# New opening for a two-layer diffusion backbone: modulation in four column bands of the PE array, in groups of 512 features, each group normalised, split and multiplied into two output tiles when it arrives

## Chip, cores, metric

One core of one Trainium2 chip. The time is the device time of one execution in microseconds; of two kernels the lower one is better. The engines have one in-order list of instructions each: PE (TensorE, matmuls), DVE (VectorE), ACT (ScalarE), POOL (GpSimd) and SP (SyncE, which here only issues DMAs). They wait for one another with semaphores.

## What is computed

Two layers over 256 latent and 256 context tokens (512 columns, T) of width 2048, all in float32:

```python
for i in range(2):
    sh_l, sc_l, g_l = split(silu(c)     @ ada_w[i] + ada_b[i], 3)   # ada_w[i]: 2048 x 6144
    sh_c, sc_c, g_c = split(silu(c_ctx) @ ada_w[i] + ada_b[i], 3)
    u_lat = rmsnorm(h_lat, norm_g[i]) * (1 + sc_l) + sh_l
    u_ctx = rmsnorm(h_ctx, norm_g[i]) * (1 + sc_c) + sh_c
    o_lat, o_ctx = mixer_i(u_lat, u_ctx)       # begins with u @ w_in (2048 x 6656, layer 1: 2048 x 4416)
    h_lat = h_lat + g_l * (o_lat @ w_out[i])   # and h_ctx in layer 0
return h_lat
```

Layer 0 mixes with windowed attention and a Hyena branch, whose filters (`z -> sin -> sin -> w3 * decay`) and their spectra don't depend on the tokens; they are made in the opening. Layer 1 mixes with two kinds of attention. What matters here is the way up to the first products `u @ w_in` of each layer.

## The kernel before

**Layout.** Tokens lie transposed, `hT[128, 16, 512]`: 16 feature tiles (k) of 128 partitions, 512 token columns. A product makes one output tile of 128 features: the weights are cast to a high part `wh` (ACT, `split_high`, L810) and a low part `wl` (DVE, `split_low`, L820), the normed input likewise to `xh` and `xl`, all of type fp32r, and PE adds `wh.xh + wh.xl` over 16 k's (L836, L839) and then `wl.xh` (L842): 48 matmuls of 512 columns. Weights arrive in `raw`, `wh` and `wl` hold two tiles each. Layer 0 has 52 tiles, its output projection 16, layer 1 has 41 slots, its projection 16 (half as wide).

**Blocks.** The program is a sequence of blocks, between which all engines wait for each other: `start_block`, `norm_block` of layer 0, `layer0_block`, `out_block`, `norm_block` of layer 1, `layer1_block`, `out_block`.

**`start_block`.** The modulation `silu(c) @ ada_w` for c and c_ctx at once. Of layer 0's 6144 columns, 2048 (the scale, chunks 2 and 3) go through PE: pieces of 128 x 1024 as the moving operand, the two conditioning vectors in 8 columns of weights (`condw`, L527), into one bank, turned to columns afterwards. The others, and layer 1's, go by chunks of 1024 columns through DVE (`ada_piece`, L338 and L350: multiply a piece by one number per partition and add, once for each vector; `ada_fold`, `ada_columns` L389 and `ada_store` L400 then sum over partitions). Chunks 0 and 1 (the shift) are done in this block, 32 pieces of 512 KB loaded by POOL (L362, a ring of two); the other eight in later blocks, two pieces per output tile. Beside that: PE turns the token rows (`xtok`) to `hT` (L519, ACT copies, L554), POOL squares and sums them (L684, L686), and four filters are made in four stages each (`filters`: matmuls with w3 L489; decay L618; sums of magnitudes L501 of `flt_abs` L560; reciprocal L635; spectra L509; scaling L642; bias L650; stores to `spectra`).

**`norm_block`.** One matmul sums the squares over partitions (L725), ACT takes the root (L732), DVE the reciprocal of 128x512 (L758). Then for each k: `ntmp = hT * nri` (POOL L720, every third on DVE L772), scale and shift (ACT, two halves, L745), cast to `xh` and difference to `xl` (DVE, L764, L766), and PE runs the products of the first tile on what arrives. SP stores `hT` as the residual, 4 MB.

Of the kernel before, what the change touches and what calls it, by code (L numbers as in the profile page):

```python
# [31 lines left out]
P = 128  # L32
D = 2048
# [44 lines left out]


# [79 lines left out]
def sbuf_map(nc):  # L159
# [44 lines left out]
    b.xtok = put("xtok", "U", 0, [P, 4, D])  # L204
    b.w3 = put("w3", "U", 32 * K, [64, 4096])
    b.decay = put("decay", "U", 48 * K, [P, 2, BW])
    b.lag = put("lag", "U", 56 * K, [P, 2, 512])
    b.hT = put("hT", "S", 0, [P, KT, T])
    b.hybias = put("hybias", "S", 32 * K, [P, 2, BW])
    b.mlpw = put("mlpw", "S", 40 * K, [64, 384])  # L210
    b.zpos, b.w1, b.w2 = b.mlpw[0:33, 0:256], b.mlpw[0:33, 256:320], b.mlpw[:, 320:384]
    b.mlp0 = put("mlp0", "S", 42 * K, [64, 256])
    b.mlp1 = put("mlp1", "S", 43 * K, [64, 256])
    b.mlp2 = put("mlp2", "S", 44 * K, [64, 256])
    b.mlp3 = put("mlp3", "S", 45 * K, [64, 256])
    b.rows = put("rows", "HL", 0, [P, 3, P])
    b.flt = put("flt", "HL", 2 * K, [P, 4, 512])
    b.flt_s = put("flt_s", "HL", 10 * K, [P, 2, 512])
    b.flt_d = put("flt_d", "HL", 14 * K, [P, 2, 512])
    b.flt_abs = put("flt_abs", "EX", 0, [P, 2, 512])  # L220
    b.condw = put("condw", "V", 2560, [P, KT, 14])
    b.adarow = put("adarow", "S", 42 * K, [8, 512])
    b.flt_inv = put("flt_inv", "HL", 20 * K, [P, 512])
    b.kstage = put("kstage", "HL", 22 * K, [P, 4, 512])
    b.ada_w_pe = put("ada_w_pe", "RAW", 0, [P, 4, 1024])

    b.nsq = put("nsq", "EX", 4 * K, [P, T])
    b.nsum = put("nsum", "EX", 6 * K, [P, T])
    b.nrs = put("nrs", "S", 32 * K, [P, T])
    b.nri = put("nri", "S", 34 * K, [P, T])  # L230
# [77 lines left out]
ADA_START = 2  # L308
ADA_PE = 2
ADA_CHUNKS = [(0, n) for n in (0, 1)] + [(0, 4), (0, 5)] + [(1, n) for n in range(6)]  # L310
# [6 lines left out]


def ada_source(ada_w, layer, n, k):
    return ada_w[layer, k * P:(k + 1) * P, n * 1024:(n + 1) * 1024]  # L320
# [36 lines left out]
def ada_load(pool, b, s, ada_w, p):  # L357

    if p >= 2:
        pool.wait_ge(s.ada_used, p - 1)  # L360
    layer, n = ADA_CHUNKS[p // KT]
    pool.dma_start(b.ada_w[:, p % 2, :], ada_source(ada_w, layer, n, p % KT)).then_inc(s.ada_landed[p % 2], 16)  # L362


def ada_fold(nc, dve, b, s, chunk):
# [4 lines left out]
    if chunk > 0:  # L370
        dve.wait_ge(s.ada_summed, chunk)
# [22 lines left out]
def ada_store(nc, dve, b, s, bank, chunk):  # L394
# [3 lines left out]
    dve.wait_ge(s.ada_summed, chunk + 1)  # L398
# [3 lines left out]
        bias.unsqueeze(1).to_broadcast([P, vecs, 8]), ALU.add).then_inc(s.ada_stored, 1)  # L402


def start_block(nc, b, s, ps, g):
# [3 lines left out]
    with block:  # L409
# [3 lines left out]
        def _(sp):  # L413
            sp.dma_start(b.core[:, 0:2 * P], g.core[:, 0:2 * P]).then_inc(s.ident_in, 16)
            sp.dma_start(b.rows[:], g.rows).then_inc(s.rows_in, 16)
            sp.dma_start(b.mlpw[:], g.mlpw).then_inc(s.rows_in, 16)
            sp.dma_start(b.sink[:], g.ev_sink.to_broadcast((P, HEADS))).then_inc(s.rows_in, 16)
            for t in range(4):
                src = (g.x, g.ctx)[t // 2][0, (t % 2) * P:(t % 2 + 1) * P, :]
                sp.dma_start(b.xtok[:, t, :], src).then_inc(s.x_in, 16)  # L420

            def store_spectra(f):

                o, c = f // 2, f % 2
                sp.wait_ge(s.k_scaled, 4 * (f + 1))
                sp.wait_ge(s.k_ready, 2 * (f + 1))
                for h in range(2):
                    sp.dma_start(g.kf_d[2 * c + h, :, o], b.kstage[:, :, 256 * h:256 * h + 256]).then_inc(s.k_out, 16)

            for n in range(KT):  # L430
                for h in range(2):
                    p = 2 * n + h
                    if p >= 4:
                        sp.wait_ge(s.ada_pe_used, p - 3)
                    sp.dma_start(b.ada_w_pe[:, p % 4, :], ada_source(g.ada_w, 0, ADA_PE + h, n)).then_inc(
                        s.ada_pe_landed[p % 4], 16)
# [29 lines left out]
        def _(pe):  # L466
# [1917 lines left out]
```

## Time and profile before

| | |
|---|---|
| median of 3 runs | 1713.72 us (1712.8 to 1721.43) |
| the profiled execution | 1720.74 us, of which span 1719.0 us |
| PE busy | 1583.7 us, 92% of the span |
| DVE, ACT, POOL busy | 1153.0, 544.2, 294.5 us |
| mean granted PE clock | 0.953 of full speed |
| DMA | 279.62 MB, 163 GB/s in the mean |

Busy time of PE includes matmuls that run at half clock or use few columns of the array, so it is to be read stage by stage.

### The profile page before, as it was taken

To read this page: it belongs to the slowest core of one execution; us is meant where nothing else is said; L and a number is where in the kernel's file an instruction comes from. 1 tells how busy PE (TensorE), PEld (TensorE's weight loads), DVE (VectorE), ACT (ScalarE), POOL (GpSimd) and SP (SyncE) were. 2 spreads that over 40 slices of the span, in tenths; PEclk is the share of its full clock that TensorE was granted. 3 is DMA by queue.
4 is the path that set the end of the run, shared out by engine and by line. 5 is a ranking of instruction groups with operands and counts; after the bars stand their busy time and mean duration, and the time that the engine had idled before them with its cause. 6 is when DMAs were issued, how large, how long until landed. Compare 5 with 4: busy or idle time off the path is not lost. (4 is left out here: it accounts for less than half of the span.)

```text
span 1719.0 us, 19161 instructions
## 1 busy us (share of the span) xinstructions
PE 1583.7 (92%) x7619; PEld 1216.7 (71%) x7619; DVE 1153.0 (67%) x1244; ACT 544.2 (32%) x742; POOL 294.5 (17%) x296
## 2 busy tenths in 40 slices
PE   4998499999999999999999899968999988899998
PEld 1322168888878877887877688844788866688998
DVE  3898879988889758668675555547457656464543
ACT  1111332222222232332322311114336555554432
POOL 0233523232223100000000044432000000000000
PEclk9988679999999999999999999986999999999999
DMA  9786645655565554454445867741244324134575
GB/s 327 242 283 229 201 147 166 191 167 182 164 191 164 172 158 136 144 157 148 130 153 189 262 209 210 218 164 48 75 112 110 98 62 117 43 98 124 153 216 147
DMA packets 303224, 279.62 MB, mean 163 GB/s; under 512 B 13472, under 2 KB 267744, under 8 KB 301408
## 3 DMA queue, kind: packets, MB, share of 16 engines
q1 hardware_dynamic: 280096, 194.50, 38.1%
q0 software_dynamic: 23040, 83.90, 14.8%
q8 instruction: 61, 1.00, 0.2%
q14 instruction: 27, 0.22, 0.0%
HBM read 257.40 MB, written 20.97 MB: 162 GB/s over the span
## 5 line engine op out<-in xcount | busy, mean ns | idle before, releaser
L836 PE MATMUL banks<-xh,wh 128*128 128x512 f32 (+1 forms) x1904 | 674.3, 369 | 42.3 <-DVE xh L764 24.7
L839 PE MATMUL banks<-xl,wh 128*128 128x512 f32 (+1 forms) x1904 | 658.2, 360 | 8.9 <-DVE xl L766 7.9
L836 PEld LDWEIGHTS banks<-xh,wh 128*128 128x128 f32 x1904 | 367.5, 193 | 110.6 <-issue 45.4
L839 PEld LDWEIGHTS banks<-xl,wh 128*128 128x128 f32 x1904 | 367.5, 193 | 77.2 <-DVE xl L766 22.5
L842 PE MATMUL banks<-xh,wl 128*128 128x512 f32 (+1 forms) x1904 | 379.2, 352 | 0.0
L820 DVE TENSOR_TENSOR wl<-raw,wh 128x2048 fp32r<-128x2048 f32 (+1 forms) x124 | 282.4, 2277 | 110.6 <-ACT wh L810 110.6
L842 PEld LDWEIGHTS banks<-xh,wl 128*128 128x128 f32 x1904 | 315.5, 191 | 47.7
L810 ACT ACTIVATE wh<-raw 128x2048 fp32r<-128x2048 f32 (+1 forms) x124 | 235.4, 1899 | 252.4 <-PE banks L842 168.5
L338 DVE SCALAR_TENSOR_TENSOR ada_acc<-ada_w,cond,ada_acc 128x1024 f32<-128x1024 f32 x150 | 199.6, 1331 | 24.8 <-DMA ada_w<-in_ada_w 22.3
L362 POOL DMA_DIRECT2D ada_w<-in_ada_w x160 | 87.1, 544 | 706.6 <-DVE ada_acc L350 512.8
L350 DVE SCALAR_TENSOR_TENSOR ada_acc<-ada_w,cond,ada_acc 128x1024 f32<-128x1024 f32 x120 | 166.2, 1385 | 0.0
L2068 DVE RECIPROCAL rs<-rs 128x256 f32<-128x256 f32 (+1 forms) x27 | 56.9, 2108 | 57.9 <-ACT rs L1984 57.8
L1621 DVE SCALAR_TENSOR_TENSOR hT<-banks,ada,hres 128x256 f32<-128x256 f32 x48 | 21.8, 481 | 108.5 <-PE banks L842 108.5
L527 PE MATMUL banks<-ada_w_pe,condw 128*8 128x512 f32 x128 | 63.9, 646 | 6.9 <-DMA ada_w_pe<-in_ada_w 6.9
L1163 ACT ACTIVATE cx<-banks,cols 128x512 f32<-128x512 f32 x16 | 12.5, 778 | 149.0 <-PE banks L842 149.0
L969 POOL TENSOR_TENSOR spec<-spec,prod 128x512 f32<-128x512 f32 x32 | 47.7, 1515 | 59.6 <-DVE prod L1303 59.6
L684 POOL TENSOR_TENSOR nsq<-hT 128x512 f32<-128x512 f32 x30 | 47.3, 1578 | 18.1 <-DVE hT L1621 17.3
L686 POOL TENSOR_TENSOR nsum<-nsum,nsq 128x512 f32<-128x512 f32 x30 | 46.0, 1532 | 2.3
L2102 DVE TENSOR_REDUCE mx<-banks 128x2 f32<-128x1024 f32 x16 | 19.6, 1224 | 38.3 <-PE banks L1891 30.5
L554 ACT ACTIVATE hT<-banks 128x512 f32<-128x512 f32 x16 | 9.6, 598 | 112.3 <-PE banks L519 112.3
L527 PEld LDWEIGHTS banks<-ada_w_pe,condw 128*8 128x8 f32 x128 | 10.8, 94 | 48.5 <-issue 41.3
L745 ACT ACTIVATE nu<-ntmp,ada,gain 128x256 f32<-128x256 f32 x64 | 34.6, 592 | 31.1 <-DVE ntmp L772 12.8
(240 smaller groups left out, 1544.5 us busy)
## 6 DMA issues: line engine op xcount, KB each, us to landing
ada_w<-in_ada_w POOLq DMA_DIRECT2D x160, 512.0 KB, 4.2
raw<-in_ev_w_in SPq DMA_DIRECT2D x52, 1024.0 KB, 7.2
raw<-in_od_w_in SPq DMA_DIRECT2D x34, 1024.0 KB, 5.6
raw<-in_w_out SPq DMA_DIRECT2D x32, 1024.0 KB, 6.4
ada_w_pe<-in_ada_w SPq DMA_DIRECT2D x32, 512.0 KB, 6.6
residual<-hT SPq DMA_DIRECT2D x2, 4096.0 KB, 14.7
spectra<-kstage SPq DMA_DIRECT2D x8, 512.0 KB, 3.9
kf<-spectra SPq DMA_DIRECT2D x4, 1024.0 KB, 4.9
```

What stands on the lines that cost most here:

```text
L338: ins = nc.vector.scalar_tensor_tensor(out=acc[:, 0, :], in0=w, scalar=b.cond[:, k, 0:1], in1=acc[:, 0, :], op0=ALU.mult, op1=ALU.add)
L350: ins = nc.vector.scalar_tensor_tensor(out=acc[:, 1, :], in0=w, scalar=b.cond[:, k, 1:2], in1=acc[:, 1, :], op0=ALU.mult, op1=ALU.add)
L362: pool.dma_start(b.ada_w[:, p % 2, :], ada_source(ada_w, layer, n, p % KT)).then_inc(s.ada_landed[p % 2], 16)
L527: last = nc.tensor.matmul(ps[7][0:8, :], b.condw[:, n, 6 - 2 * q:14 - 2 * q], b.ada_w_pe[:, p % 4, 512 * x:512 * x + 512], start=(p == 0 a ...
L684: nc.gpsimd.tensor_tensor(b.nsq[:], x, x, ALU.mult).then_inc(s.squared, 1)
L810: nc.scalar.activation(b.wh[:, t % 2, 0:width], b.raw[:, t % 2, 0:width], ACT.Copy).then_inc(s.hi_done, 1)
L820: nc.vector.tensor_tensor(b.wl[:, t % 2, 0:width], b.raw[:, t % 2, 0:width], b.wh[:, t % 2, 0:width].bitcast(F32), ALU.subtract).then_inc( ...
L836: nc.tensor.matmul(out, wh[:, k, :], b.xh[:, seg, k, :], start=(k == 0), stop=False)
L839: nc.tensor.matmul(out, wh[:, k, :], b.xl[:, seg, k, :], start=False, stop=False)
L842: last = nc.tensor.matmul(out, wl[:, k, :], b.xh[:, seg, k, :], start=False, stop=(k == KT - 1))
L969: nc.gpsimd.tensor_tensor(b.spec[:, j], b.spec[:, j], b.prod[:, j % 2, :].rearrange("p (v c) -> p v c", v=2), ALU.subtract if j % 2 == 0 e ...
L2068: v.reciprocal(b.rs1[:, 0:width], b.rs1[:, 0:width]).then_inc(s.odd_rstd, 1)
```

## The change

- `start_block` loads layer 0's scale and shift (4096 columns) in 32 pieces of 1 MB, laid out beforehand so that every partition's part is one run of 8 KB: eight groups of 512 output columns, four pieces each, first the scale and then the shift of the features 0 to 511, then of the next 512. A piece has four k's; PE multiplies k number q of it into PSUM partitions 32q to 32q+31 (`ada_matmuls`), so a group's sum lies in four bands; ACT copies it to `arow`, and four small matmuls with `quads` turn it and add the bands (`ada_turn`). DVE adds the bias and makes the gain (`modulation`). Nothing of layer 0's scale and shift goes through DVE's sums any more.
- The work is written out by ticks, one per piece. The four filters start at ticks 2, 6, 11 and 15, a stage a tick; their magnitudes are also summed in bands. The spectra are stored unscaled, the inverse of the magnitude sums (128x4 a filter) is applied where layer 0 mixes; the bias is added to one row of the filter.
- Tokens are laid out as `hT` beforehand and loaded by POOL. ACT squares them at ticks 4 and 5, PE sums them (`square_sums`), the root and the reciprocal are taken of 128x4 and spread by PE into a bank; DVE multiplies `hT` by it in place.
- Group by group ACT shifts four k's (ticks 9, 17, 25 and at the end), DVE splits them, and PE adds them to two output tiles at once (`pair_product`): k's 0 to 11 at ticks 22 to 28, 12 to 15 at the end. `layer0_block` therefore starts its products at tile 2 (`if i > 1`), and the weights of tile 2 are split in the opening.
- `norm_block` is left for layer 1 alone: root and reciprocal of 128x4, spread by PE; DVE scales, ACT shifts and also casts to `xh`, DVE makes `xl`; PE makes tiles 0 and 1 together.
- All weight tiles of both layers and of both output projections are laid out beforehand, so that a tile is one run of 8 KB per partition and not 16 of 512 bytes. The residual of layer 0 is read from the input; its store is gone.

```diff
+def modulation_tiles(a):
+    first = a["ada_w"][0][:, :2 * D].reshape(4, 4, P, 2, 4, 512)
+    first = first.transpose(4, 3, 0, 2, 1, 5)[:, ::-1]
...
+FILTER_TICK = (2, 6, 11, 15)
+SQUARE_TICK = 4
+SPLIT_TICK = 20
+PAIR_TICK = {22: (0, 1), 23: (2, 3), 24: (4, 5), 25: (6, 7), 27: (8, 9), 28: (10, 11)}
+SCALE_TICK = {7: range(0, 6), 8: range(6, 12), 9: range(12, 16)}
...
+            for p in range(ADA_PIECES):
+                if p >= 3:
+                    sp.wait_ge(s.ada_pe_used, p - 2)
+                sp.dma_start(b.ada_ring[:, p % 3].rearrange("p k n -> p (k n)"), g.ada_first[p]).then_inc(
+                    s.ada_pe_landed[p % 3], 16)
...
+                if p == 12:
+                    load_raw(sp, b, s, 0, l0_weights(g, 0), (KT, P))
+                if p == 20:
+                    sp.wait_ge(s.flt_sd, 12)
+                    load_raw(sp, b, s, 1, l0_weights(g, 1), (KT, P))
...
+            def ada_matmuls(p):
+                grp, r = divmod(p, 4)
+                pe.wait_ge(s.ada_pe_landed[p % 3], 16 * (p // 3 + 1))
+                if r == 0 and grp > 0:
+                    pe.wait_ge(s.row_kept, rows_kept("ada", grp - 1))
+                for q in range(4):
+                    last = nc.tensor.matmul(ps[7][32 * q:32 * q + 32, :], b.condw[:, 4 * r + q, :], b.ada_ring[:, p % 3, q, :],
+                                            start=(r == 0), stop=(r == 3), skip_group_check=True)
+                last.then_inc(s.ada_pe_used, 1)
...
+            for tick in range(ADA_PIECES):
+                ada_matmuls(tick)
+                if tick == 0:
+                    pe.wait_ge(s.curved, 2)
+                    nc.tensor.matmul(ps[3][0:64, 0:256], b.w2, b.mlp3[:], start=True, stop=True).then_inc(s.mlp_mm, 1)
+                if tick % 4 == 0 and tick > 0:
+                    ada_turn(tick // 4 - 1)
+                if filter_stage(tick) is not None:
+                    filters(*filter_stage(tick))
+                if tick in (SQUARE_TICK, SQUARE_TICK + 1):
+                    for k in range(8 * (tick - SQUARE_TICK), 8 * (tick - SQUARE_TICK) + 8):
+                        square_sums(k)
...
+                if tick in PAIR_TICK:
+                    pe.wait_ge(s.norm_scaled, KT)
+                    pe.wait_ge(s.norm_root, 1)
+                    pe.wait_ge(s.hi_done, 2)
+                    pe.wait_ge(s.lo_done, 2)
+                    for k in PAIR_TICK[tick]:
+                        for i in range(2):
+                            pair_product(nc, pe, b, s, 0, i, k, ps[i], k + 1, k + 1)
+            ada_turn(ADA_GROUPS - 1)
+            for i in range(2):
+                for k in range(KT - 4, KT):
+                    last = pair_product(nc, pe, b, s, 0, i, k, ps[i], k + 1, k + 1)
+                last.then_inc(s.proj_done, 1)
...
+            for tick in range(ADA_PIECES):
...
+                if tick % 8 == 1 and tick > 8:
+                    shift(tick // 8 - 1)
+                if tick == SPLIT_TICK:
+                    act.wait_ge(s.k_out, 128)
+                    split_high(nc, act, b, s, 0)
+                    split_high(nc, act, b, s, 1)
...
+def pair_product(nc, pe, b, s, t, i, k, bank, high, low):
+    out = bank.rearrange("p (v t) -> p v t", t=256)
+    wh = b.wh[:, (t + i) % 2, :].rearrange("p (k m) -> p k m", m=P)
+    wl = b.wl[:, (t + i) % 2, :].rearrange("p (k m) -> p k m", m=P)
+    pe.wait_ge(s.norm_high, high)
+    nc.tensor.matmul(out, wh[:, k, :], b.xh[:, :, k, :], start=(k == 0), stop=False)
+    nc.tensor.matmul(out, wl[:, k, :], b.xh[:, :, k, :], start=False, stop=False)
+    pe.wait_ge(s.norm_low, low)
+    return nc.tensor.matmul(out, wh[:, k, :], b.xl[:, :, k, :], start=False, stop=(k == KT - 1))
...
 def l0_weights(g, i):
     col = l0_tile(i)[1]
-    return g.ev_w_in[0, :, col:col + P].rearrange("(k p) n -> p k n", p=P)
+    return g.ev_tiles[col // P].rearrange("p (k n) -> p k n", k=KT)
...
-                if i > 0:
+                if i > 1:
                     product(nc, pe, b, s, i, ps[i % 2])
...
-                    v.tensor_tensor(out, out, gate, ALU.mult).then_inc(s.mixed, 1)
+                    v.scalar_tensor_tensor(out=out, in0=out, scalar=b.inv_sum[:, o, 2 * grp + c:2 * grp + c + 1], in1=gate,
+                                           op0=ALU.mult, op1=ALU.mult).then_inc(s.mixed, 1)
```

## Rows read from the trace of the kernel before

**Rows 1.** Busy time by stage: us, then each engine busy (x), PEclk, DMA share, GB/s.

```profile
22.60:187.20 164.60, 138.14 (x337) 43.57 (x337) 131.31 (x122) 19.56 (x34) 55.70 (x59) 0.90 0.70 239
...
187.20:234.80 47.60, 29.19 (x50) 13.72 (x50) 36.95 (x41) 22.87 (x36) 17.31 (x11) 0.53 0.52 173
...
234.80:1141.90 907.10, 888.65 (x4020) 711.38 (x4020) 652.46 (x697) 231.60 (x282) 199.82 (x205) 0.99 0.58 176
...
1141.90:1193.50 51.60, 29.78 (x52) 14.07 (x51) 36.07 (x42) 21.14 (x36) 19.01 (x13) 0.57 0.24 92
```

**Rows 2.** Groups of instructions of the opening, 22.6 to 187.2 us: busy us, mean ns, idle before.

```profile
L527 PE MATMUL banks<-ada_w_pe,condw 128*8 128x512 f32 x128 | 63.9, 646 | 6.9 <-DMA ada_w_pe<-in_ada_w 6.9
...
L350 DVE SCALAR_TENSOR_TENSOR ada_acc<-ada_w,cond,ada_acc 128x1024 f32<-128x1024 f32 x29 | 38.6, 1332 | 0.0
...
L338 DVE SCALAR_TENSOR_TENSOR ada_acc<-ada_w,cond,ada_acc 128x1024 f32<-128x1024 f32 x28 | 36.6, 1309 | 21.9 <-DMA ada_w<-in_ada_w 21.7
...
L489 PE MATMUL banks<-w,mlp 64*128 64x512 f32 x32 | 21.8, 839 | 10.1 <-DVE kstage L642 10.1
...
L560 ACT ACTIVATE flt_abs<-flt 128x512 f32<-128x512 f32 x16 | 9.7, 626 | 15.5 <-PE banks L501 12.1 <-DVE flt L618 3.4
```

**Rows 3.** Timeline of PE: start us, us, instruction and count.

```profile
142.27 3.60 PE L527 MATMUL banks<-ada_w_pe,condw 128*8 128x512 f32 x8
...
150.85 7.19 PE L489 MATMUL banks<-w,mlp 64*128 64x512 f32 x8 [4.98 <-DVE kstage L642]
...
234.83 0.47 PE L836 MATMUL banks<-xh,wh 128*128 128x512 f32 x1 [0.32 <-PEq L698]
...
245.81 0.39 PE L836 MATMUL banks<-xh,wh 128*128 128x512 f32 x1
```

**Rows 4.** Timeline of ACT and PE in the norm of layer 1.

```profile
1147.76 1.28 ACT L732 ACT_TABLE_LOAD   x1 [15.09 <-PEq L1507]
...
1147.80 2.04 PE L725 MATMUL banks<-nsum,core 128*128 128x512 f32 x2 [5.86 <-PEq L1507]
...
1158.67 0.76 PE L836 MATMUL banks<-xh,wh 128*128 128x512 f32 x1 [8.83 <-DVE xh L764]
...
1187.53 5.64 PE L842 MATMUL banks<-xh,wl 128*128 128x512 f32 x16
...
1193.50 0.47 PE L836 MATMUL banks<-xh,wh 128*128 128x512 f32 x1 [0.32 <-PEq L698]
```

**Rows 5.** Duration of one, min/median/max ns, of L389 over the run; timeline of eight.

```profile
L389 PE MATMUL banks<-ada_part,quads x80: 176/197/237, 141.5 to 1130.7; 128*32 128x16 f32 x64, 128*32 128x8 f32 x16
...
141.49 0.26 PE L389 MATMUL banks<-ada_part,quads 128*32 128x16 f32 x8
```

**Rows 6.** Groups of instructions of layer 0, 234.8 to 400 us.

```profile
L820 DVE TENSOR_TENSOR wl<-raw,wh 128x2048 fp32r<-128x2048 f32 x12 | 27.3, 2279 | 0.0
...
L810 ACT ACTIVATE wh<-raw 128x2048 fp32r<-128x2048 f32 x13 | 24.8, 1909 | 0.0
```

**Rows 7.** Groups of instructions of the norm of layer 0, 187.2 to 234.8 us.

```profile
L745 ACT ACTIVATE nu<-ntmp,ada,gain 128x256 f32<-128x256 f32 x32 | 17.3, 591 | 13.3 <-DVE xl L766 6.7 <-DVE ntmp L772 6.4
...
L766 DVE TENSOR_TENSOR xl<-nu,xh 128x512 fp32r<-128x512 f32 x16 | 14.9, 931 | 0.5
...
L764 DVE CAST xh<-nu 128x512 fp32r<-128x512 f32 x16 | 11.0, 690 | 0.7 <-ACT nu L745 0.2
```

**Rows 8.** Busy time in stretches of 10 us, columns as in rows 1.

```profile
10.00:20.00 10.00, 2.28 (x5) 0.57 (x4) 8.96 (x21) 1.93 (x3) 1.19 (x2) 1.00 1.01 422
...
20.00:30.00 10.00, 7.63 (x16) 2.02 (x16) 3.52 (x5) 1.61 (x3) 0.53 (x1) 1.00 1.02 247
```

**Rows 9.** Waits of PE (us, times, longest); DMA issues, KB each, us to landing.

```profile
PE banks L836 <- ACT wh L810: 7.3, 3, 4.2
...
raw<-in_ev_w_in SPq DMA_DIRECT2D x52, 1024.0 KB, 7.2
...
kf<-spectra SPq DMA_DIRECT2D x4, 1024.0 KB, 4.9
```

More of the change, by code:

```diff
@@ L402, in ada_store, with filter_stage, rows_kept @@
         bias.unsqueeze(1).to_broadcast([P, vecs, 8]), ALU.add).then_inc(s.ada_stored, 1)
+FILTER_TICK = (2, 6, 11, 15)
[3 more added lines that the diff above has]
+SCALE_TICK = {7: range(0, 6), 8: range(6, 12), 9: range(12, 16)}
+def filter_stage(tick):
+    for f, first in enumerate(FILTER_TICK):
+        if first <= tick < first + 4:
+            return f, tick - first
+    return None
+def rows_kept(kind, n):
+    order = []
+    for tick in range(ADA_PIECES):
+        if tick == SQUARE_TICK + 1:
+            order.append(("square", 0))
+        if filter_stage(tick) is not None and filter_stage(tick)[1] == 1:
+            order.append(("filter", filter_stage(tick)[0]))
+        if tick % 4 == 3:
+            order.append(("ada", tick // 4))
+    return order.index((kind, n)) + 1
 def start_block(nc, b, s, ps, g):
@@ L501, in filters @@
[L501 to L507 removed]
+                        last = nc.tensor.matmul(ps[2][32 * i:32 * i + 32, :], b.ones[:, 0:32], b.flt_abs[:, i, :], start=True,
+                                                stop=True, skip_group_check=True)
@@ new lines, in filters @@
+                    last.then_inc(s.flt_sum, 1)
+                if stage == 2:
+                    pe.wait_ge(s.row_kept, rows_kept("filter", f))
+                    nc.tensor.matmul(ps[3][0:1, :], b.quads[:, 0:1], b.sabs[:], start=True, stop=True)
+                    for i in range(4):
+                        last = nc.tensor.matmul(ps[2][:, i:i + 1], b.sabs[:, P * i:P * i + P], b.quads[:, 0:1], start=True,
+                                                stop=True)
+                    last.then_inc(s.flt_sum, 1)
+                    pe.wait_ge(s.core_in, 48)
+                    pe.wait_ge(s.flt_sd, 3 * f + 2)
+                    for m in (1, 3):
@@ new lines, in _ @@
+            for tick in range(ADA_PIECES):
+                if tick % 4 == 0 and tick > 0:
+                    modulation(tick // 4 - 1)
+                if filter_stage(tick) is not None:
+                    filters(*filter_stage(tick))
+                if tick == SQUARE_TICK + 2:
+                    dve.wait_ge(s.norm_root, 1)
+                    v.reciprocal(b.nri[:, 0:4], b.nrs[:, 0:4]).then_inc(s.norm_rstd, 1)
+                for k in SCALE_TICK.get(tick, ()):
+                    dve.wait_ge(s.norm_spread, 1)
+                    v.tensor_tensor(b.hT[:, k, :], b.hT[:, k, :], ps[0], ALU.mult).then_inc(s.norm_scaled, 1)
+                if tick % 8 == 1 and tick > 8:
+                    split(tick // 8 - 1)
+                if tick == SPLIT_TICK:
+                    split_low(nc, dve, b, s, 0)
+                    split_low(nc, dve, b, s, 1)
@@ L723, in _ @@
         @blk.tensor
         def _(pe):
-            nc.tensor.matmul(ps[6], b.ones, b.nsum[:], start=True, stop=True).then_inc(s.norm_summed, 1)
-            product(nc, pe, b, s, t, ps[(t - T1 if layer else t) % 2],
-                    ready=(s.norm_high, s.norm_low, base(KT)))
+            for j in range(4):
+                last = nc.tensor.matmul(ps[6][:, j:j + 1], b.nsum[:, j * P:(j + 1) * P], b.ones[:, 0:1], start=True, stop=True)
+            last.then_inc(s.norm_summed, 1)
+            pe.wait_ge(s.norm_rstd, 3)
@@ L729, in _ @@
+            last.then_inc(s.proj_done, 1)
+            for k in range(KT - 4, KT):
+                last = pair_product(nc, pe, b, s, t, 1, k, ps[1], KT + k + 1, KT + k + 1)
+            last.then_inc(s.proj_done, 1)
         @blk.scalar
         def _(act):
-            act.wait_ge(s.norm_summed, base(1) + 1)
-            nc.scalar.activation(b.nrs[:], ps[6], ACT.Sqrt, scale=1.0 / D, bias=b.small[:, 0:1]).then_inc(s.norm_root, 1)
-            if layer == 0:
-                split_high(nc, act, b, s, t)
```

573 lines of the change are left out of this document (294 added, 279 removed).

## The prediction

> **What bounds the kernel now.** I read the granted clock and the busy time stage by stage first, then the groups of instructions in the opening, then its timeline, then the waits of PE. The table by stage [rows 1] shows two kinds of stage. From 234.8 to 1141.9 us PE is busy for 888.65 of 907.10 us at a clock of 0.99: the weight tiles run back to back, and only fewer columns would shorten them. The opening (0 to 187.2 us) and the two norm stages (47.6 us and 51.6 us, clock 0.53 and 0.57) are not like this. In the opening DVE is busy for 131.31 of 164.60 us after the first 22.6; PE looks busy for 138.14, but rows 2 show what with: modulation matmuls of 8 columns, filters, transposes. DVE's largest groups are the modulation sums of 1.3 us, two for each piece of 512 KB [rows 2], and its idle time goes to the wait for those same pieces (21.7 us).
>
> The points to hold on to are in [rows 3]: the second tile of layer 0 starts at 234.83 us, the third at 245.81 us; a full tile at full clock is thus 10.98 us for 48 matmuls with what stands between, 0.229 us each. The changed kernel makes tiles 0 and 1 inside its opening, so what counts is when its tile 2 starts, against 245.81. Likewise tile 2 of layer 1: before, tile 1 starts at 1193.50 [rows 4], so tile 2 at 1204.5.
>
> **What the change removes.** The sums on DVE for chunks 0 and 1 (32 pieces, 64 operations of about 1.3 us, some 82 us of DVE [rows 2]), the token transposes, POOL's squares in the opening, the four broad reciprocals, the scalings of the spectra and the 4 MB residual store of layer 0. The norm stage of layer 0, from 187.2 to 234.8, goes as a stage. All this lay on the path, since the opening was one in-order list on DVE.
>
> **What PE gets in its place.** 32 pieces of 1 MB, each four f32 matmuls of 512 columns, into four 32-column bands. A f32 matmul is two instructions; eight of them took 3.60 us [rows 3], that is 0.43 us from start to start and 0.59 us for the last. What four bands cost together is the unknown of this change. Bounds: if bands do not overlap, 8 x 0.43 = 3.44 us a piece; if all four run at once, two passes, 0.87 us. The nearest row is the fold of the modulation sums, which already writes four bands: eight matmuls of about 197 ns in 0.26 us, so (260 - 197) / 7 = 9 ns from start to start [rows 5]. They have 16 columns, so they can't say much of 512, but they do overlap. As PE starts its instructions in order and the two passes of a matmul need the same band, pass 2 of band 0 holds back band 1; then only the second pass of one and the first of the next overlap, and a piece costs 4 x 0.43 = 1.72 us. I take this middle value. The Trainium skill ("TensorE: Matmul & The Clock Gate", Part 3) says of tiles in the array that matmuls in different column groups run concurrently and start some 4 ns apart; by it a piece would cost about 0.87 us, which is the first rival below. Rows 5 agree with it as far as starts 9 ns apart go.
>
> PE's list in the opening, with p for the cost of a piece. Each of four filters: 8 instructions for the filter (3.44), four banded sums of magnitudes (p), a row sum and small turns (1.2), 16 instructions of spectra (6.9): 11.5 + p. That is 46 + 4p. Pieces: 32p. Tiles 0 and 1: 96 matmuls of 0.229 = 22. Turns of the modulation rows, the spread of the norm: 4. Sum 72 + 36p = 134 us with p = 1.72.
>
> Time in which PE waits, or works slower:
> - Start: conditioning vector, two sine chains on DVE and w3 and decay behind other loads: as before, stage 0 of filter 0 can't start before about 20 us; two pieces (3.4 us) are done by then. +20 - 3.4.
> - Low clock after this idle start: eight such instructions took 7.19 us after a wait of 4.98 [rows 3], not 3.6. +4.
> - Squares: ACT makes 16 of 0.63 us (the magnitude's row in [rows 2]) with a ring of four, PE waits for each: +8 beyond what it does meanwhile.
> - The square root behind a table load (1.28 us, [rows 4]) ahead of filter 1's magnitudes: +2.5. Filters 1 to 3, the wait for the magnitudes: +3.
> - Spectra must be stored before wh may be written (they share memory), then two casts of 1.9 us and two differences of 2.28 us [rows 6]: PE reaches tick 22 about 5 us too early. +5.
> - After the last piece: row copy, turn, bias, shift, cast, about 3.5 us, then four feature tiles at DVE's pace (cast and difference, 0.43 and 0.69 without disturbance; the means of 690 and 931 ns in [rows 7] hold long ones while POOL works, and POOL is idle here), 1.25 us each, of which PE's own work fills half: +5.
>
> 134 + 16.6 + 4 + 8 + 2.5 + 3 + 5 + 5 = 178 us. Is it the transfers instead? All that moves up to there is about 48 MB (33.5 modulation, 4.2 tokens, 4.2 spectra written, 3.1 weights, 3.3 others); at the 410 to 422 GB/s of [rows 8] that is 116 us. So PE, not DMA, sets the pace, and the ring of three hides the load, at p = 1.72. DVE has about 75 us of work and ACT about 60 in the same time (the groups of rows 2 and 7 at their means, over what the new lists hold).
>
> Behind it: split_low of tile 2 ends some 1.5 us after PE, the block change costs 0.5, and tile 2 now waits for the drain of tile 0 (ACT 0.8, DVE twice 0.75), which before lay beneath tile 1's product: +2.4. Tile 3's low half then comes after the pieces of tiles 0 and 1 on DVE, about as PE asks for it: nothing. Tile 2 starts at about 182.5: 245.8 - 182.5 = **63 us gained**.
>
> **The norm of layer 1.** Before: block at 1147.8, first product at 1158.67, tile 0 done about 1193.2, tile 1 starts at 1193.50 [rows 4]. After: the reciprocal of 128x4 in place of 128x512 (3.35 us) and a spread through PE; ACT does one cast of 1.9 us first. First product about 1156.5. Each feature tile then costs ACT two shifts of 0.59 [rows 7] and a cast of 0.6: 1.85 us, the same pace as before (1158.7 to 1187.5 over 16 is 1.8), but two tiles are made on it: six matmuls of 0.229 fit in 1.85. PE ends near 1188, split_low of tile 2 near 1190, the drain of tile 0 takes 1.2: tile 2 starts at 1192, against 1204.5: **12 us gained**. If ACT's pace were 2.2, it would be 7.
>
> **Contiguous weights.** PE waits 7.3 us in three places for wh, there behind a late raw load. A 1 MB load with short rows lands in 7.2 us, one with rows of 8 KB (kf) in 4.9 [rows 9]. I take **3 us**, between 0 and 7. Elsewhere raw is two tiles ahead and hidden by 10.98 us of product. The extra 1.5 MB of core and the scalar in the mixing are hidden by the same.
>
> **Sum.** 63 + 12 + 3 = 78. The profiled execution took 1720.74 us (span 1719.0 and 1.7 around it); it becomes 1642.5. The median of the runs is 7.0 us below the profiled one, so I forecast 1635.5 for it.
>
> **Rivals.**
> 1. *All four bands at once* (p = 0.87): 36 x 0.85 = 31 us less, of which 5 go to waits for pieces in the ticks without a filter: 1635 - 26 = **1609**. For it: the starts 9 ns apart in [rows 5]. Against it: the order of the two passes.
> 2. *Bands one after another* (p = 3.44): 36 x 1.72 = 62 more, 8 of it under the waits above: **1689**. For it: no row with 512 columns overlaps.
> 3. *Transfers bound the opening*: in one stretch the queues were full at 247 GB/s [rows 8]. 48 MB at that rate are 195 us, and a tail of 13: 208 for 178, **1665**. Against it: those 10 us held w3 (64 partitions) and small constants, and the pieces are long rows.
> 4. *Slower*: bands one after another, and the clock at its lower level (1.2 of 2.4 GHz) while PE waits for pieces and partners: the norm stages show clocks of 0.53 and 0.57 where PE idles between matmuls [rows 1]. A piece then costs 6.9 us. From 1689 it takes 25 us to reach the old time, and 34 us to be 0.5% slower: from ten such pieces on it decides; twelve give **1730**. Against it: a PE so loaded is not idle, and at full load the clock was 0.99.
> 5. *The new order buys nothing*: the in-order lists of the opening wait on each other (a filter's stages are spread over PE, ACT, DVE and PE again) as much as DVE's work cost before: **1715**.
>
> **How the numbers follow.** Forecast (p near 1.7) 0.38, rival 1 0.25, rival 2 0.19, rival 3 0.08, rival 4 0.06, rival 5 0.04. The range reaches from rival 1 with a little more in the stalls (1600) to rival 2 (1692). A measurement tells 0.5% (9 us) from no change. Faster 0.90, same 0.04, slower 0.06.
>
> **What would show it.** The banded matmuls: 128 pairs of them, and whether a group of eight in the timeline lasts about 0.9, 1.9 or 3.6 us. The start of tile 2's product at 180 to 185 us. PE waiting for squares near 40 to 50 us and for wl before the pair products. Layer 1: first pair product near 1156 - 63, and 1.85 us a feature tile at full clock. The stage from tile 2 of layer 0 to the last projection of out 0 as long as before less a few us. I am wrong if PE idles for pieces in the filter ticks (rival 3), if the clock in the opening is much below 0.9 (rival 4), or if tile 2 of layer 0 starts well late for lack of its low half.

## The result and the profile after

The changed kernel takes 1656.58 us (median of four runs, 1652.35 to 1661.13), the kernel before beside it 1716.13 (1712.8 to 1721.43). The ratio is 0.9651, 95% interval [0.9605, 0.9696]: about 60 us faster. The forecast was 1635, the range 1600 to 1692. The profiled execution took 1660.79 us (span 1659.0) against 1720.74 (span 1719.0).

First the table of busy time by stage, of the changed kernel, cut at the start of tile 2 of layer 0 (203.5), the last product of out 0 (1101.0), and the start of tile 2 of layer 1 (1147.4), and below it two stretches within the opening. Columns as in [rows 1].

```profile
0.00:203.50 203.50, 154.64 (x639) 66.06 (x639) 72.44 (x128) 62.86 (x105) 11.17 (x21) 0.91 0.66 240
203.50:1101.00 897.50, 879.93 (x3972) 703.20 (x3972) 648.05 (x695) 228.24 (x279) 198.71 (x203) 0.99 0.53 179
1101.00:1147.40 46.40, 31.82 (x115) 22.58 (x115) 27.32 (x39) 33.04 (x57) 2.30 (x2) 0.82 0.28 104
1147.40:1659.00 511.60, 481.14 (x3104) 421.18 (x3102) 280.99 (x313) 242.01 (x347) 0.00 (x0) 0.98 0.34 118
...
16.70:53.00 36.30, 29.70 (x84) 9.90 (x84) 10.12 (x19) 6.09 (x11) 0.00 (x0) 1.00 0.78 315
...
95.00:110.00 15.00, 14.92 (x43) 4.91 (x43) 6.21 (x10) 3.63 (x7) 1.49 (x2) 0.54 0.78 269
```

The same cuts in the kernel before:

```profile
0.00:245.80 245.80, 182.33 (x445) 68.17 (x446) 185.36 (x196) 48.64 (x76) 77.29 (x81) 0.84 0.70 239
245.80:1142.00 896.20, 877.71 (x3973) 702.26 (x3971) 647.45 (x693) 229.01 (x280) 198.18 (x202) 0.99 0.57 174
1142.00:1205.20 63.20, 41.44 (x101) 23.53 (x101) 39.25 (x44) 24.53 (x40) 19.01 (x13) 0.65 0.32 108
1205.20:1719.00 513.80, 482.23 (x3103) 422.74 (x3101) 280.89 (x313) 241.98 (x348) 0.00 (x0) 0.98 0.41 113
```

Row by row the gain is 42.3 us in the opening, -1.3 in layer 0 and out 0, 16.8 in the norm of layer 1 and 2.2 behind it: 60.0 in all. DVE is busy for 72.44 us of the opening, where it was 185.36: it is no longer what sets the pace. Nothing to speak of that was gained is given back later. The question is why the opening gave 42 and not 63.

The groups of PE in the opening, 0 to 203.5 us (busy us, mean ns, idle before), against [rows 2]:

```profile
L521 PE MATMUL banks<-ada_ring,condw 128*32 128x512 f32 x256 | 41.2, 702 | 14.9 <-DMA ada_ring<-in_ada_first 11.6 <-ACT arow L692 3.3
L553 PE MATMUL banks<-w,mlp 64*128 64x512 f32 x32 | 20.8, 807 | 2.8 <-ACT kstage L638 2.8
L572 PE MATMUL banks<-flt_d,lag 128*128 128x512 f32 x32 | 16.5, 665 | 0.0
L966 PE MATMUL banks<-xh,wh 128*128 128x512 f32 x32 | 15.0, 468 | 13.5 <-DVE wl L954 11.6 <-DVE xh L795 1.9
L579 PE MATMUL banks<-flt_s,lag 128*128 128x512 f32 x32 | 14.8, 605 | 0.0
...
L531 PE MATMUL banks<-quads,arow 128*128 128x2 f32 x64 | 10.1, 279 | 0.7 <-ACT arow L692 0.7
...
L558 PE MATMUL banks<-flt_abs,core 128*32 128x512 f32 x32 | 6.7, 931 | 1.4 <-ACT flt_abs L672 1.4
L563 PE MATMUL banks<-sabs,quads 128*1 128x512 f32 x8 | 5.6, 797 | 0.0
L565 PE MATMUL banks<-quads,sabs 128*128 128x1 f32 x32 | 5.0, 279 | 0.0
L605 PE MATMUL banks<-core,nri 128*128 128x128 f32 x8 | 2.0, 436 | 0.0
```

(Neighbouring matmuls overlap at their ends, so these busy times add up to more than the 154.64 us of the table. Where small terms are added up below, I count each instruction from its start to the start of the next.)

The timeline of PE in the same stretch, against [rows 3] (start us, us, instruction and count, in brackets the idle time before it and its releaser):

```profile
21.61 1.93 PE L521 MATMUL banks<-ada_ring,condw 128*32 128x512 f32 x8 [1.90 <-DMA ada_ring<-in_ada_first]
...
28.44 7.19 PE L553 MATMUL banks<-w,mlp 64*128 64x512 f32 x8
...
42.77 1.87 PE L531 MATMUL banks<-quads,arow 128*128 128x2 f32 x8
...
77.17 2.03 PE L605 MATMUL banks<-core,nri 128*128 128x128 f32 x8
79.13 1.06 PE L521 MATMUL banks<-ada_ring,condw 128*32 128x512 f32 x8
...
123.76 1.07 PE L521 MATMUL banks<-ada_ring,condw 128*32 128x512 f32 x8
124.76 1.05 PE L531 MATMUL banks<-quads,arow 128*128 128x2 f32 x8
...
133.99 3.70 PE L579 MATMUL banks<-flt_s,lag 128*128 128x512 f32 x8
...
156.52 0.77 PE L966 MATMUL banks<-xh,wh 128*128 128x512 f32 x1 [11.57 <-DVE wl L954]
...
191.80 0.79 PE L966 MATMUL banks<-xh,wh 128*128 128x512 f32 x1 [1.91 <-DVE xh L795]
...
203.52 0.79 PE L984 MATMUL banks<-xh,wh 128*128 128x512 f32 x1 [4.29 <-DVE cz L1416]
```

Three readings. First, the four bands of a piece (L521, eight instructions) take 1.07 us from the start of the first to the end of the last; eight unbanded ones with 512 columns too take 3.70 (L579). Second, the same groups have two durations: pieces 1.93 and 1.07, turns of a row (L531) 1.87 and 1.05, filters (L553) 7.19 and 3.70. These are the two levels of the clock. The low one holds up to about 53 us, where the clock column still says 1.00, again from about 75 to 79 and from 95 to 109 (there the column says 0.54), and for some 4 us behind the waits at 156.5 and 191.8. This matters for reading the sign that was named for a piece: 1.93 us looks like the middle value (about 1.9), but it is four bands at once at the low clock, and only the 1.07 further on tells the two apart. Third, one wait of 11.57 us stands before the pair products. The timelines of ACT, POOL and DVE show what it hangs on:

```profile
140.35 1.49 POOL L499 DMA_DIRECT2D spectra<-kstage  x2 [18.71 <-ACT kstage L638]
...
149.83 3.71 ACT L944 ACTIVATE wh<-raw 128x2048 fp32r<-128x2048 f32 x2 [9.29 <-DMA spectra<-kstage]
...
151.77 4.49 DVE L954 TENSOR_TENSOR wl<-raw,wh 128x2048 fp32r<-128x2048 f32 x2 [8.63 <-ACT wh L944]
```

The last spectra are issued at 140.35 and have landed at 149.83; then come two casts and, overlapping, two differences, and PE starts at 156.52. The same stores landed faster in the kernel before, where SP issued them and not POOL (DMA issues before, then after):

```profile
spectra<-kstage SPq DMA_DIRECT2D x8, 512.0 KB, 3.9
...
spectra<-kstage POOLq DMA_DIRECT2D x8, 512.0 KB, 8.3
```

Whether the queue or the traffic beside them makes the 4.4 us was not tested.

The norm of layer 1 in the timeline of all engines, against [rows 4]:

```profile
1106.78 1.84 PE L853 MATMUL banks<-core,nsum 128*128 128x1 f32 x8 [5.85 <-PEq L1658]
...
1108.15 1.89 ACT L944 ACTIVATE wh<-raw 128x2048 fp32r<-128x2048 f32 x1
...
1110.46 2.08 PE L857 MATMUL banks<-core,nri 128*128 128x128 f32 x8 [1.83 <-DVE nri L899]
...
1115.19 0.77 PE L966 MATMUL banks<-xh,wh 128*128 128x512 f32 x1 [2.66 <-ACT xh L887]
...
1147.40 1.42 PE L984 MATMUL banks<-xh,wh 128*128 128x512 f32 x1
```

From the block's first matmul to the first pair product it takes 8.41 us (before 10.87: 1147.80 to 1158.67), to tile 2 it takes 40.62.

### The profile page after: what moved, and what is told of

Read it like the earlier page. It is cut to its first block and busy times, and to the rows that moved or that the text cites. A ratio compares the mean times of both kernels' runs of the same rounds, so it can differ in the third digit from the quotient of the medians.

```text
span 1659.0 us, 19427 instructions
## 1 busy us (share of the span) xinstructions
PE 1547.5 (93%) x7827; PEld 1213.0 (73%) x7827; DVE 1028.8 (62%) x1174; ACT 566.1 (34%) x787; POOL 212.2 (13%) x226
## 5 line engine op out<-in xcount | busy, mean ns | idle before, releaser
L984 PE MATMUL banks<-xh,wh 128*128 128x512 f32 (+1 forms) x1840 | 638.2, 363 | 16.5 <-ACT wh L944 4.8
L987 PE MATMUL banks<-xl,wh 128*128 128x512 f32 (+1 forms) x1840 | 620.9, 353 | 0.3 <-DVE xl L1762 0.2
L987 PEld LDWEIGHTS banks<-xl,wh 128*128 128x128 f32 x1840 | 351.6, 191 | 54.6 <-issue 5.3
L990 PE MATMUL banks<-xh,wl 128*128 128x512 f32 (+1 forms) x1840 | 360.8, 349 | 0.0
L365 DVE SCALAR_TENSOR_TENSOR ada_acc<-ada_w,cond,ada_acc 128x1024 f32<-128x1024 f32 x120 | 159.5, 1329 | 6.5 <-DMA ada_w<-in_ada_rest 4.4
L388 POOL DMA_DIRECT2D ada_w<-in_ada_rest x128 | 70.2, 549 | 629.1 <-DVE ada_acc L377 404.8
L377 DVE SCALAR_TENSOR_TENSOR ada_acc<-ada_w,cond,ada_acc 128x1024 f32<-128x1024 f32 x90 | 126.4, 1404 | 0.0
L521 PE MATMUL banks<-ada_ring,condw 128*32 128x512 f32 x256 | 41.2, 702 | 14.9 <-DMA ada_ring<-in_ada_first 11.6
L966 PE MATMUL banks<-xh,wh 128*128 128x512 f32 x64 | 29.0, 453 | 17.4 <-DVE wl L954 11.6
L1998 PE MATMUL banks<-sq,core 128*128 128x256 f32 (+1 forms) x74 | 31.1, 504 | 15.0 <-ACT sq L2128 7.8
L2145 ACT ACTIVATE prob<-banks,nb 128x512 f32<-128x512 f32 x32 | 21.7, 683 | 41.9 <-DVE nb L2256 41.9
```

The source lines that it names most:

```text
L365: ins = nc.vector.scalar_tensor_tensor(out=acc[:, 0, :], in0=w, scalar=b.cond[:, k, 0:1], in1=acc[:, 0, :], op0=ALU.mult, op1=ALU.add)
L377: ins = nc.vector.scalar_tensor_tensor(out=acc[:, 1, :], in0=w, scalar=b.cond[:, k, 1:2], in1=acc[:, 1, :], op0=ALU.mult, op1=ALU.add)
L388: pool.dma_start(b.ada_w[:, p % 2, :], ada_rest[p // KT, p % KT]).then_inc(s.ada_landed[p % 2], 16)
L521: last = nc.tensor.matmul(ps[7][32 * q:32 * q + 32, :], b.condw[:, 4 * r + q, :], b.ada_ring[:, p % 3, q, :], start=(r == 0), stop=(r == 3 ...
L984: nc.tensor.matmul(out, wh[:, k, :], b.xh[:, seg, k, :], start=(k == 0), stop=False)
L987: nc.tensor.matmul(out, wh[:, k, :], b.xl[:, seg, k, :], start=False, stop=False)
```

## The experiments

Each ratio is to runs of the kernel before made beside it: 1716.13 us beside the changed kernel, 1718.1 beside experiments 1 to 4, 1719.19 beside 5 to 8; so I compare ratios where these meet. The changed kernel's ratio is 0.9651, with a wide interval [0.9605, 0.9696], 8 us to either side, which every difference from it inherits.

**1. The four bands in one.** All sixteen conditioning blocks of a group go into band 0 of the array and add up there. The sum over the bands is then made by the accumulation, and the other bands hold zeros.

```diff
-                    last = nc.tensor.matmul(ps[7][32 * q:32 * q + 32, :], b.condw[:, 4 * r + q, :], b.ada_ring[:, p % 3, q, :],
-                                            start=(r == 0), stop=(r == 3), skip_group_check=True)
+                    last = nc.tensor.matmul(ps[7][0:32, :], b.condw[:, 4 * r + q, :], b.ada_ring[:, p % 3, q, :],
+                                            start=(r == 0 and q == 0), stop=(r == 3 and q == 3), skip_group_check=True)
...
+            chain(v.memset(ps[7], 0.0))
```

> The changed kernel with one thing undone: all four k's of a piece go into PSUM partitions 0 to 31 of the bank (one band), the other three are zero. Same loads, same number of matmuls. If the bands run at once (the trace of the changed kernel: eight instructions in 1.06 us at the high clock, 1.93 at the low one), each piece now lasts 8 x 0.43 = 3.6 us, 2.4 more at the high clock; 32 pieces are 77 us, of which about 12 hide under PE's waits for pieces: tile 2 of layer 0 starts near 203 + 65 = 268 us, span near 1724. If the overlap in that trace is only how ends are modelled, the span stays near 1659. If PE then is busier and its clock stays high longer, some 10 us less than 1724.

1703.32 us in its one run, span 1701.5. The group of the pieces (groups of PE, 0 to 246 us):

```profile
L521 PE MATMUL banks<-ada_ring,condw 128*32 128x512 f32 x256 | 119.6, 615 | 9.6 <-DMA ada_ring<-in_ada_first 7.3 <-ACT arow L692 2.3
...
L985 PE MATMUL banks<-xh,wh 128*128 128x512 f32 x2 | 1.4, 710 | 4.3 <-DVE cz L1417 4.3
```

119.6 us for 41.2, one piece 3.62 us in its timeline: the bands are what makes pieces cheap. The mean of one instruction (615 ns) is not longer than with bands (702, a mean that holds many at the low clock): what bands change is only how many run at once. But tile 2 starts at 244.87, that is 41.4 us later and not 65 as expected, let alone 78. From start to start the pieces cost 76.5 us more. Of this 21 us come back from PE's waits (48.9 us to 27.9), for the wait for the stored spectra (11.6 us) is gone, as PE comes late enough, and 14 us from the other groups, most of which now run at full clock, which is up for the most part from about 21 us on. So these losses of the changed kernel are there because PE has too little to do.

**2. The splits before the last stores.** The staging buffer of the spectra is two tiles, the odd one away from wh; the splits of tiles 0 and 1 wait for the even one's stores only, which were issued a filter earlier.

```diff
-    b.kstage = put("kstage", "HL", 0, [P, 2, 4, 512])
+    b.kstage = [put("kstage0", "HL", 0, [P, 4, 512]), put("kstage1", "C", 2 * K, [P, 4, 512])]
...
-                        s.k_out, 16)
+                        (s.k_out, s.k_odd)[f % 2], 16)
...
-                    act.wait_ge(s.k_out, 128)
+                    act.wait_ge(s.k_out, 64)
```

> The staging buffer of the odd filters moves to memory that is free until layer 0 (the part of core that is loaded later), so the casts of the first two weight tiles wait for the stores of filter 2 and no longer for those of filter 3, and filter 3's copies no longer wait for filter 2's stores. Theory that the wait at tick 22 (11.57 us) is part of the shortfall: PE reaches the pair products at about 144 and waits some 2 us for wl, tile 2 starts 9 to 11 us earlier, span near 1649. Rival, that transfers take the place of the wait: seven pieces of 1 MB are still to come behind tick 24, at 2.6 to 3.3 us each; PE waits for them and 3 us or less are gained. Rival, low clock: less than 2 us.

1645.48 us (1640.8 to 1650.2), ratio 0.9587 [0.9565, 0.9608]; span 1639.0. PE's waits in the opening of this run:

```profile
PE banks L522 <- DMA ada_ring<-in_ada_first: 11.7, 6, 3.4
...
PE banks L967 <- DVE wl L955: 1.1, 1, 1.1
```

The wait of 11.6 us is down to 1.1, and the other waits of the opening stand within 1 us. The profiled execution (the fastest of the four) starts tile 2 at 186.45, 17 us earlier and not 9 to 11; but in it the clock also rose before 40 us where it had risen near 53, so not all of the 17 belongs to the edit. The ratios give 11 us, about what the wait was worth. The two intervals just touch, so by times alone this gain is barely told from nothing; experiment 4 settles it.

**3. Warming matmuls.** 35 matmuls of 128x512 that nobody reads (0.9 us each at full clock), into free banks, where PE waits in the opening: 18 before and in the first ticks, 11 before the pair products, the rest one or two at a time.

```diff
+            def warm(count, bank=0):
+                for _ in range(count):
+                    nc.tensor.matmul(ps[bank], b.ident, b.core[:, 0:512], start=True, stop=True)
...
             for tick in range(ADA_PIECES):
+                warm({0: 4, 1: 3, 2: 4, 3: 4, 4: 1, 20: 1}.get(tick, 0), 1 if tick > 8 else 0)
                 ada_matmuls(tick)
```

> The changed kernel with 40 more f32 matmuls of 512 columns on PE (identity times constants, into a bank that is written later), placed where PE waits: before the rows land, before ticks 0 to 4, in ticks 7, 11, 20 and 22 and before the last pair products. Nothing else changes. Theory that the low clock is the larger part of the shortfall: banded groups last 1.06 us and not 1.93 from the first tick on, the stretch from tick 3 to the end of the squares (36 to 65.6 us) shrinks to some 18 us, that from 95 to 113 us to 12, tile 2 of layer 0 starts 15 to 20 us earlier, near 185, span near 1641. Rival, that loads and the other engines set the pace there anyhow: under 5 us. If the extra matmuls only delay PE, it becomes slower by up to 5 us.

1646.41 us (1644.01 to 1648.47), ratio 0.9582 [0.9565, 0.9599]; span 1644.0. Groups of PE, 0 to 189.3 us:

```profile
L526 PE MATMUL banks<-ada_ring,condw 128*32 128x512 f32 x256 | 35.6, 614 | 3.4 <-DMA ada_ring<-in_ada_first 3.0 <-ACT arow L701 0.5
...
L558 PE MATMUL banks<-w,mlp 64*128 64x512 f32 x32 | 14.8, 602 | 0.8 <-ACT kstage L647 0.8
L536 PE MATMUL banks<-quads,arow 128*128 128x2 f32 x64 | 8.4, 254 | 0.7 <-ACT arow L701 0.7
```

The expectation speaks of 40 matmuls, the edit has 35. 38.2 us of useless work made the kernel 10 us faster by the medians, 12 by the ratios. The same instructions as in the table above cost 35.6 for 41.2, 14.8 for 20.8, 8.4 for 10.1; tile 2 starts at 189.37 for 203.52, 14 us earlier where 15 to 20 were expected. The work fitted into waits: PE's for pieces fell from 11.6 to 3.0 and the one for wl went under the eleven. Even so the low level came back for some 4 us behind the turns, where eight instructions of the spectra took 5.38 us and not 3.68:

```profile
42.85 5.38 PE L577 MATMUL banks<-flt_d,lag 128*128 128x512 f32 x8
```

**4. Both** (edits 2 and 3, with two warming matmuls in place of eleven before the pair products).

> Both of the last two edits (with 2 in place of 11 extra matmuls in tick 22). If clock and store wait are independent parts of the shortfall, their gains add: tile 2 starts near 175 to 180, span 1632 to 1637. If transfers become the bound (48 MB at the 410 us/MB-rate seen in full stretches, 2.6 us a piece), it gains 5 us less than the sum, and PE's idle time before the banded matmuls goes to the pieces.

1639.93 us (1635.97 to 1641.91), ratio 0.9542 [0.9523, 0.9562]; span 1639.1, tile 2 at 179.06. (The 410 us/MB of the expectation is meant as 410 GB/s.) Its interval lies below those of experiments 2 and 3, so each edit gains on top of the other, 7 to 8 us; and they mostly add: 11 and 12 us alone, 18.7 together by the ratios (0.0109 x 1716). The span is 1639.1, a little above the 1632 to 1637 expected: it is only 19.9 below the changed kernel's where tile 2 starts 24.5 earlier; 3.1 us of that are longer waits for wh in layer 0 and out 0 (7.9 for 4.8).

**5. The old norm stage of layer 1** in the changed kernel: DVE's reciprocal of 128x512 and its casts, tile 0 alone made on the fly.

```diff
-            for k in range(KT):
-                for i in range(2 if k < KT - 4 else 1):
-                    last = pair_product(nc, pe, b, s, t, i, k, ps[i], KT + k + 1, KT + k + 1)
...
+            nc.tensor.matmul(ps[6], b.ones, b.nsum[:], start=True, stop=True).then_inc(s.norm_summed, 1)
+            product(nc, pe, b, s, t, ps[(t - T1 if layer else t) % 2],
+                    ready=(s.norm_high, s.norm_low, base(KT)))
```

> The changed kernel, with the norm stage of layer 1 of the kernel before (reciprocal of 128x512, casts on DVE, tile 0 alone made on the fly, tile 1 as a full product). Theory: the 16.8 us by which that stage is shorter in the changed kernel (63.2 to 46.4 us) come from its own new order and are kept to the end: 1656.6 + 17 = 1673 us, and 63 us from the last product of out 0 to tile 2 of layer 1. Rival: they come from something else (clock, other landings) or are given back later: 1657 to 1662 us.

1674.76 us (1672.29 to 1679.85), ratio 0.9744 [0.9722, 0.9766], 16 us more by the ratios. The stage, from the last product of out 0 to tile 2 of layer 1 (table by stage):

```profile
1099.40:1162.00 62.60, 40.79 (x100) 23.28 (x100) 39.26 (x44) 24.00 (x38) 19.01 (x13) 0.65 0.28 109
```

62.60 us for 46.40, with the clock and the busy times of before. The whole gain of this stage is the new order's, and none of it is given back. Which part of the new order (the small reciprocal, the cast on ACT, two tiles at once) makes how much was not tested.

**6. Short rows for the weight tiles** (512 bytes, as before) in the changed kernel.

```diff
-    return g.ev_tiles[col // P].rearrange("p (k n) -> p k n", k=KT)
+    return g.ev_w_in[0, :, col:col + P].rearrange("(k p) n -> p k n", p=P)
```

> The changed kernel, with the weight tiles of ev_w_in, od_w_in and w_out again read in rows of 512 bytes. Theory: PE waited 7.3 us for wh before and 4.8 after, and xh 5.6 and 4.4, so that the long rows are worth 2 to 4 us: 1659 to 1661 us, a 1 MB load of a weight tile landing in about 7.2 us, not 6.0. Rival one: two tiles ahead hide it all, 1656 to 1657. Rival two: with 4.5 times as many packets the pieces of modulation land later in the opening too: 1665 or more.

1661.52 us (1659.49 to 1663.56), ratio 0.9659 [0.9641, 0.9677]: 1.4 us by the ratios, well inside the interval. The view of the DMAs:

```profile
DMA packets 295339, 274.41 MB, mean 165 GB/s; under 512 B 12945, under 2 KB 262993, under 8 KB 289617
...
raw<-in_ev_w_in SPq DMA_DIRECT2D x52, 1024.0 KB, 6.4
```

With 4.4 times as many packets a tile lands in 6.4 us, not 6.0, and PE waits 7.5 us for wh in layer 0 and out 0, not 4.8. That agrees with a gain of 2 to 3 us, but the times can't tell it from nothing. Short rows make only 0.4 of the 1.2 us by which a tile landed later in the kernel before (7.2 us, [rows 9]); what made the rest was not tested.

**7. More warming, between stages.** On top of experiment 4: two such matmuls at the end of the opening and two at the head of layer 0, five behind out 0, four in the norm of layer 1.

```diff
+            warm(2, 2)
...
+            for _ in range(2):
+                nc.tensor.matmul(ps[2], b.ident, b.core[:, 0:512], start=True, stop=True)
             for i in range(L0_TILES):
```

> The kernel with warming matmuls and early splits, with further such matmuls (0.9 us each at full clock) into free banks where PE idles between stages: four between tile 1 and tile 2 of layer 0 (idle 4.3 us), five after the last product of out 0, four in the norm stage of layer 1. Theory: after each of these waits PE runs 12 to 16 matmuls at 0.43 us in place of 0.23, so 3 us come back at tile 2 of layer 0 and about 3 at the norm of layer 1: 1639.9 - 6 = 1634 us. Rival: the products there are paced by ACT and DVE, and the added matmuls delay what waits behind them: 1639 to 1642.

1638.11 us (1633.92 to 1641.69), ratio 0.9526 [0.9504, 0.9548], beside 0.9542 [0.9523, 0.9562]: not told apart. The timeline of PE and its waits show why:

```profile
177.91 0.50 PE L999 MATMUL banks<-xh,wh 128*128 128x512 f32 x1 [0.41 <-DVE cz L1433]
...
1089.60 0.47 PE L981 MATMUL banks<-xh,wh 128*128 128x512 f32 x1 [1.18 <-ACT xh L902]
```

```profile
PE banks L1146 <- POOL fold L1126: 5.1, 1, 5.1
```

Both places now start at the full clock (0.50 and 0.47 us for 0.79 and 0.77). Tile 2 of layer 0 starts 1.15 us earlier, but a little behind it stands POOL's fold, for which PE waits 5.1 us where it waited 2.0. In the norm of layer 1 the first pair product comes 8.33 us after the block's first matmul, as without (8.41), and ACT's shift and cast set 1.65 us for each feature tile, full clock or not. The rival was right in kind: a faster PE buys nothing where another engine sets the pace.

**8. The turns issued twice**, on top of experiment 4: the eight of the modulation rows, and the two kinds in each filter.

```diff
-                for j in range(4):
+                for j in (0, 1, 2, 3, 0, 1, 2, 3):
                     last = nc.tensor.matmul(ps[6][:, 8 * grp + 2 * j:8 * grp + 2 * j + 2],
```

> The kernel with warming matmuls and early splits, with each turn of a row into columns issued twice: the eight of the modulation (8.4 us in all), the four of the filter sums (4.2 us) and the four row sums beside them (4.1 us). Theory: the small matmuls lie on PE's list, which sets the end of the opening, and cost what the lines say: 1639.9 + 15 to 17 = 1656 us, tile 2 of layer 0 15 to 17 us later than at 179.1. Rival: PE has slack there (waits for pieces, magnitudes and splits), and less than half is seen: 1640 to 1647 us.

1650.46 us (1646.23 to 1650.88), ratio 0.9593 [0.9575, 0.9611]: 8.8 us more than experiment 4 by the ratios. Tile 2 in the timeline:

```profile
191.77 0.70 PE L995 MATMUL banks<-xh,wh 128*128 128x512 f32 x1 [4.27 <-DVE cz L1427]
```

12.7 us later than at 179.06. The 16.7 us of the expectation are busy times of the groups, in which neighbours' ends count twice; from start to start the doubled instructions add 14.2 us (29.3 for 15.1), so nine tenths of their time lie on the path, and the waits for pieces took in some of the rest (3.1 to 1.8). The span rose by 10.0 us: behind tile 2 the kernel ran 2.7 us shorter than in experiment 4. My number was 15 to 17, so the theory holds in kind and was too high in size.

## Why the prediction was right, and where it was off

**The mechanism** was right: DVE's sums were the path, PE took their place, and tile 2 starts earlier. That the sums were the path is read from the profile before (DVE busy for 131.31 of 164.60 us, [rows 1]); no run puts them back, and none divides the opening's 42 us among its parts. 60 us came, 78 were forecast. The step that was off is PE's list in the opening: its terms were mis-sized in both directions, and the time came out as near as it did because two large errors partly cancel, which is luck.

The forecast had tile 2 at 182.5 us, measured 203.5. The terms, counted from start to start; "at full clock" is by the timeline of experiment 3, without its two short stretches at the low level:

- *A piece, p.* 1.72 us was put in; measured at full clock it is 1.00 (123.76 to 124.76). The 32 pieces and four sums of magnitudes cost 34.8 us where I had 61.9. **-27.** Rival 1's mechanism was the true one. The argument against it, that the second pass of a band holds back the next band, is refuted by it. The rule of the Trainium skill ("TensorE: Matmul & The Clock Gate", Part 3), that matmuls in different column groups run concurrently, agrees with this; the price estimated by it was 0.87 us. Experiment 1 shows the price of the alternative: 119.6 / 32 = 3.74 us a piece. The squares, put at 8 us, cost 8 (7 of matmuls, 1.4 of waits).
- *Small matmuls.* I had 4.8 us for row sums and turns of the filters and 4 for the modulation's turns and the spread, 8.8 in all. At full clock they cost 17.3. **+9.** A turn has one or two columns, but loads 128x128 float32 weights eight times for 1.05 us.
- *Other work at full clock.* The filter matmuls and spectra were 43.5 for 41.4, **+2**; the products of tiles 0 and 1 were 25.0 for 22, mostly because the last four feature tiles come at DVE's pace, **+3**.
- *The low clock.* I had 4 us. PE is busy for 154.6 us with what at full clock takes 129; of the difference one us is the first transposes' (next term), and 24 are left. **+20.** I priced one group behind one wait; in fact PE ran at the low level up to about 53 us, again from 75 to 79 and from 95 to 109, and twice behind waits.
- *The front.* Filter 0 was to start at 20 us; it starts at 28.44, for PE waits for each of the first three pieces (4.9, 1.9 and 3.0 us). Waits and the first transposes and sine products are 22.8 us for 16.6. **+6.** Here it is the transfers that set the pace (these pieces beside the other first loads), and work put into these waits kept the clock up (experiment 3).
- *The other waits.* 23.5 for 15.5. **+8.** The wait for the split was 11.6 and not 5, as the stores of the spectra take 8.3 us to land and I counted the casts and differences alone. The drain of tile 0 ahead of tile 2 was named and is there (4.29 us together with block change and low half, for 4.4).

These sum to -27 + 9 + 2 + 3 + 20 + 6 + 8 = 21 us.

**The norm of layer 1** gave 16.8 us for 12, and experiment 5 shows that the new order makes all of it. First product and pace were nearly as computed (8.41 us after the block's first matmul, for 8.7; 1.65 us a feature tile for 1.85): 16 x 0.2 = 3.2 of the 4.8 us are ACT's pace.

**Contiguous weights** were put at 3 us. The profile shows 2.5 us less wait for wh, the stretches of layer 0 and behind it together 0.9 us less, and experiment 6 1.4 us: not told from zero.

**The rivals.** One is right in mechanism and missed in time (1609), for what it gave was eaten by the clock, the waits and the small matmuls, which I had in no rival. Two is refuted as what the kernel does; as a price it was 1689, and experiment 1 gave 1703. Three is refuted for the opening as a whole: it moved 240 GB/s, experiment 4 took 179 us for the same loads at a mean of 272; but the first 28 us do wait for pieces. Four needed both: no piece was serial, while the low clock did come, and cost 24 us. Five is refuted by 42.3 us.

What stays open: why the clock rose before 40 us in the profile of experiment 2 and near 53 in the changed kernel's, with the same instructions up to there; why it fell at 43 us in experiment 3 and not in experiment 4; and how much of the 8.8 us between the pairs of the changed kernel's runs (1652.4 and 1661) is that, as the only trace is of a run of 1661.

## What to carry over

When work moves to an engine, price all that it is given at the rate of its own weight loads and starts, small matmuls too, and ask at which clock it will run: here a list whose front waits 20 of its first 28 us ran at half the clock up to 53 us. Matmuls with 32 columns of weights belong side by side in the array, with 512 moving columns (1.07 us for 3.62) as with 16 ([rows 5]). And once an engine has slack, look for the store or split that waits for the end of an earlier phase only because two buffers share memory: here it was worth about 11 us.

## What the runs showed of the hardware

- Four float32 matmuls of 128x32 weights and 512 columns in four column bands, eight instructions, take 1.07 us at full clock and 1.93 at the low one; in one band 3.62 at full clock. An instruction by itself lasts 588 to 617 ns at full clock either way, and about 1060 at the low one.
- A float32 matmul with 128x128 weights and two columns takes 0.26 us at full clock (four in 1.05), 0.47 at the low one; with 512 columns it takes 0.9 (four in 3.70).
- Useless matmuls in waits raised the clock and made the kernel faster by 10 to 12 us (experiment 3).
- The clock column says 1.00 from 16.7 to 53 us of the changed kernel, where eight filter instructions take 7.19 us and not 3.70. In the opening the durations tell the level, not the column.
- A 512 KB store of spectra issued by POOL took 8.3 us to land in the median, where SP's loads of twice the size take 4.8 to 6.4 in the same run, and where the same stores issued by SP took 3.9 in the kernel before.
